# An encoder step on 8 cores: the first w_in chunk loaded as fp32 over a hardware queue and cast on chip, and three SBUF places exchanged

## What is computed

```python
# sub-layer 1: mixing
proj = rmsnorm(x, g_mix_pre) @ w_in            # (T, 2048) = [u | B | C | h], 4 x 512
y_pool = pool_mix(u)                           # trailing means over 2, 4, 8, 16 rows, minus u; then w_pool
y_conv = B * conv3(C * h)                      # causal depthwise convolution of width 3
x = x + rmsnorm(concat(group_rmsnorm(y_pool), group_rmsnorm(y_conv)) @ w_out, g_mix_post)
# sub-layer 2: cross-attention into 256 memory tokens, k = m @ w_k, v = m @ w_v
s = (rmsnorm(x, g_x_pre) @ w_q) @ k.T / 16
x = x + rmsnorm((softmax(s) @ v) @ w_co, g_x_post)
# sub-layer 3: squared-ReLU MLP
x = x + rmsnorm(relu(rmsnorm(x, g_ff_pre) @ w_up)**2 @ w_down, g_ff_post)
```

## Time and profile before

| | us |
|---|---|
| median of 3 runs | 855.21 |
| lowest and highest run | 854.38 and 895.62 |
| the profiled execution, its own time | 856.95 |
| its span (first to last instruction, slowest core, number 5) | 855.4 |
| spans of the eight cores in it | 846.5 to 855.4 |
| PE, DVE, ACT, POOL busy on core 5 | 816.9, 389.1, 389.9, 85.1 |

### The profile page before, as it was taken

The page is one execution under the profiler, slowest core; times in us unless marked ns, Lnnn a source line. Parts: engine busy times, 40 slices in busy tenths (PEclk is TensorE's granted clock), DMA queues, the critical chain, the costliest instruction groups (busy, mean ns, idle before and its releaser), DMA issues.

```text
span 855.4 us, 13864 instructions; the slowest of 8 cores (846.5 to 855.4 us)
## 1 busy us (share of the span) xinstructions
PE 816.9 (96%) x4724; PEld 393.0 (46%) x4724; DVE 389.1 (45%) x538; ACT 389.9 (46%) x806; POOL 85.1 (10%) x164
## 2 busy tenths in 40 slices
PE   2899999999998999999999999999999999999996
PEld 1444454544543455445554454444444444444442
DVE  3797885569774667665222222241122322222112
ACT  3596786858774657575332223332233401233111
POOL 7522103012100001000010000000000000000000
PEclk9999999999998999999999999999999999999998
DMA  8999349720299506993789816881248820294001
GB/s 190 196 221 217 129 142 209 116 37 1 33 146 144 192 12 211 159 174 76 147 143 159 188 60 145 151 149 51 98 105 150 157 57 25 65 154 77 25 25 49
DMA packets 29792, 102.38 MB, mean 120 GB/s; under 512 B 2386, under 2 KB 13266, under 8 KB 24348
## 3 DMA queue, kind: packets, MB, share of 16 engines
q0 software_dynamic: 19408, 67.32, 45.9%
q1 hardware_dynamic: 9740, 32.75, 11.1%
q10 hardware_dynamic: 576, 1.44, 0.6%
HBM read 144.38 MB, written 18.07 MB: 190 GB/s over the span
## 4 chain that ended last, share of the span: by engine, by line
PE 84%; DMA 11%; POOL 2%; issue 1%; DVE 1%; ACT 1%; POOLq 0%; DVEq 0%; ACTq 0%
PE ps L660 81%; DMA wdn_140<-w_down 4%; DMA wco<-w_co 4%; DMA win<-w_in 3%; PE ps L665 2%; DMA up_131<-w_up 1%; POOL sAB_101 L698 0%; POOL win L734 0%; DVE X L715 0%; DVE z_99 L715 0%; ACT rf_108 L689 0%; DVE Am L725 0%; POOL se_71 L727 0%; DVE O_55 L696 0%; DVE xT_53 L696 0%
## 5 line engine op out<-in xcount | busy, mean ns | idle before, releaser
L689 ACT ACTIVATE sqj<-ps 128x1024 bf16<-128x1024 f32 (+1 forms) x33 | 32.8, 995 | 176.4 <-PE ps L660 174.2
L660 PE MATMUL ps<-xT_53,win 128*128 128x512 bf16 x256 | 62.4, 385 | 17.7 <-DMA win<-w_in 16.6
L696 DVE TENSOR_TENSOR O_56<-ps,gp 128x1024 f32<-128x1024 f32 x24 | 29.3, 1222 | 97.7 <-PE ps L660 58.8
L696 DVE TENSOR_TENSOR O_55<-ps,gp 128x1024 f32<-128x1024 f32 (+1 forms) x25 | 29.5, 1178 | 95.4 <-PE ps L660 72.6
L689 ACT ACTIVATE rt_129<-ps 128x512 bf16<-128x512 f32 x64 | 38.2, 597 | 72.2 <-PE ps L660 69.3
L689 ACT ACTIVATE rt_128<-ps 128x512 bf16<-128x512 f32 x64 | 38.2, 597 | 70.3 <-PE ps L660 69.3
L660 PE MATMUL ps<-xT_54,win 128*128 128x512 bf16 x256 | 59.5, 379 | 0.6 <-DVE O_55 L696 0.6
L660 PEld LDWEIGHTS ps<-xT_53,win 128*128 128x128 bf16 x256 | 24.4, 99 | 46.1 <-issue 21.4
L660 PE MATMUL ps<-xT_54,up_130 128*128 128x512 bf16 x192 | 42.4, 379 | 0.0
L660 PE MATMUL ps<-xT_53,up_131 128*128 128x512 bf16 x192 | 42.4, 379 | 0.0
L660 PEld LDWEIGHTS ps<-xT_54,win 128*128 128x128 bf16 x256 | 24.8, 98 | 29.9 <-issue 0.8
(11 more groups left out here) (333 smaller groups left out, 1461.8 us busy)
## 6 DMA issues: line engine op xcount, KB each, us to landing
up_130<-w_up POOLq DMA_DIRECT2D x11, 1024.0 KB, 8.5
up_131<-w_up POOLq DMA_DIRECT2D x11, 1024.0 KB, 9.8
up_132<-w_up POOLq DMA_DIRECT2D x10, 1024.0 KB, 8.9
x<-X SPq DMA_DIRECT2D x16, 512.0 KB, 3.4
X<-x SPq DMA_DIRECT2D x16, 512.0 KB, 4.2
yp<-X SPq DMA_DIRECT2D x15, 512.0 KB, 2.6
X<-xp POOLq DMA_DIRECT2D x8, 512.0 KB, 44.0
X<-xp SPq DMA_DIRECT2D x8, 512.0 KB, 4.3
```

Source lines behind the costliest of these rows:

```text
L660: P.add([("pe", lambda e, L: e.matmul(L(out), lhsT=lhsT, rhs=rhs, start=start, stop=stop, skip_group_check=True), max(0.03, n * 0.000421 + ...
L689: return e.activation(out=L(out), in_=L(in_), func=func, scale=scale, **kw)
L696: opts.append(("dve", lambda e, L: e.tensor_tensor(out=L(out), in0=L(in0), in1=L(in1), op=op), c_dve(n, per)))
```

## The change

The first chunk of `w_in` is no longer loaded and cast by POOL's queue. It comes as fp32 over the SP queue into `Or[0]` and is cast into `win` by DVE or ACT, whichever the planner takes. The four XT loads change sides: 0 and 2 go over the ACT queue, 1 and 3 over SP. The second piece of `w_in` is emitted ahead of `Xe`. In the plan the engines are taken to be free from 0.6 us on, POOL from 3.5 us on. In cross-attention `Bm` moves to A0+56K, `wq` to 82K, `wco` to 40K (over chunks 8 to 15 of `win`), and `hid` 2 and 3, `wdn` 0 and 1 follow.

```diff
@@ schedule
-        free = {e: 0.0 for e in self.ENGS}
+
+        free = {e: 3.5 if e == "pool" else 0.6 for e in self.ENGS}
@@ build_program, SBUF places
-    Bm = at("Bm", A0 + 40 * K, 8 * D, BF16)
-    wq = at("wq", A0 + 56 * K, 8 * D, BF16)
-    wco = at("wco", A0 + 82 * K, 8 * D, BF16)
+    Bm = at("Bm", A0 + 56 * K, 8 * D, BF16)
+    wq = at("wq", A0 + 82 * K, 8 * D, BF16)
+    wco = at("wco", A0 + 40 * K, 8 * D, BF16)
...
-    hparts = [at("hid%d" % i, A0 + o * K, 8 * TN, BF16) for i, o in enumerate((72, 16, 40, 48))]
+    hparts = [at("hid%d" % i, A0 + o * K, 8 * TN, BF16) for i, o in enumerate((72, 16, 56, 64))]
...
-              for i, o in enumerate((A0 + 56 * K, A0 + 64 * K, W0, W0 + 8192, A0, A0 + 8 * K, A0 + 24 * K, A0 + 32 * K))]
+              for i, o in enumerate((A0 + 40 * K, A0 + 48 * K, W0, W0 + 8192, A0, A0 + 8 * K, A0 + 24 * K, A0 + 32 * K))]
@@ build_program, the first loads
-    load_win(0)
+    load(Or[0][:, :], win_d[0, :, 0:1024], 524288)
+    copy(win[:, 0:1024], Or[0][:, :], eng="act dve", per=0.56)
     for i in range(4):
-        load(XT[i], xt0[i], 524288, q=("sp", "act")[i % 2])
+        load(XT[i], xt0[i], 524288, q=("act", "sp")[i % 2])
     load_consts()
+    load_win(1)
     load(Xe[0:NX, :], xe[:, :], NX * 4096, q="pool")
-    load_win(1)
     load_wpool()
```

## The result

The changed kernel takes 861.43 us in the median of its runs (860.89 to 862.67), beside 854.8 for the kernel before on the same chip. The ratio is 1.0084, with a 95% interval of 1.0064 to 1.0103. Ratios and intervals leave out executions more than 1.5% above the fastest of the same kernel, such as the 895.62 of the kernel before. The forecast was 852.0 with a range of 846 to 857, so the time lies outside it, on the slower side. The profiled execution of the changed kernel took 862.67 us.

The account below looks back on a forecast made before the run. Core 5 sets the metric, losing 6.7 us at w_co; the start has several limits, then DVE carries it. Span 855.4 - 4.9 (places) - 0 (start) = 850.5, plus 1.55 around it, gives 852.0 us; range 846.0 to 857.0.

Parts of the forecast that it names:

- Places of w_co, w_q, Bm: Before `fold_b`: w_co issued at about 219 or 224, its wait gone on every core, metric 4.9 us lower.
- Forecast against the median: Whole kernel: 852.0 us against the median of 855.21, a gain of 3.2 us (0.4%).
- The gain of 4.9: Slowest core's span: core 5 loses its 6.7 us at w_co, core 2 becomes slowest, 855.4 - 850.5 = 4.9 us.
- The start at 0: First loads: `r0` and `U` 1.4 us later, covered by DVE's 1.43 us idle before 29.27; 0 gained.
- the start slips: Rival at the first loads: XT 2 lands at 20.7, stage starts 4.0 us later, 856.0 us; chance 0.16.
- the sign of that rival: At the start: `U` after 28 us would show that the start slips.
- issue order and plan times: Every engine's order after the new `free` times: unreadable from a trace, allowed 2 us either way.
- Something in the new order that none of these holds: Remaining case, anywhere in the new order, outside the forecast and its rivals; no size given, chance 0.06.
- an order that opens a long stall with its lower clock: Whole kernel: reason given for a result slower by more than about 2% (17 us); chance 0.03.
- The result within 2%: Whole kernel: time within about 2% (17 us), which a measurement can't tell from no change; chance 0.96.

Follow-up runs that it names:

- e12_add_first: Changed kernel with one exchange in VectorE's order, the first addition of squares ahead of the first scaling of XT 2: 862.66 us, ratio 1.0064 to the kernel before.

## Why the prediction was wrong, step by step

- **Places of w_co, w_q, Bm: right in mechanism, half in size.** The issue moved to 224.1 on core 5 (forecast 219 or 224). On the other cores of the changed kernel it is at 224.8 to 231.5, because all that stands ahead is late; with the places alone it is at 219.3 to 222.7 everywhere. The wait is gone on every core, the fold takes 7.1 us, and on core 5 the clock stays up. Forecast against the median was 0.4%; alone it gave 0.2% [0.07, 0.31]. The gain of 4.9 was read from the spans of one execution, in which core 5 happened to be the one that waits; another core is the slowest as soon as core 5 is mended.
- **The start at 0: right in the time, not in the chain.** Landings 7.2 and 16.7 forecast, 6.9 and 16.9 seen in the first uses on core 7; the cast took 0.72 us where 0.75 was taken from the earlier trace rows. New loads in the old order: 1.0002, with `U` at 26.4 in the median as forecast. The rival "the start slips" named XT 2 at 20.7, and this didn't come. But in the changed kernel's own order three additions follow XT 2 and not two, `U` comes at 27.6 in the median, and past 28 on two cores, which the prediction had named as the sign of that rival. The slip came from the order and not from XT; taking it back gained nothing (`e12_add_first`).
- **The step that failed is "issue order and plan times".** It was said that this can't be read from a trace, and then a bound of 2 us was put on it from the largest other waits, 1.0 us each. The new order alone measured 0.8% (1.0080), about 7 us. The bound was wrong in kind. A wait that is 1.0 us in an order that fits says nothing of the waits in one that doesn't: it is the order that keeps them at 1.0. In its place the runs showed two waits of PE: one of 2.0 us at 65 to 70 us on every core, behind a copy on DVE, and one of up to 3.6 us for w_v, each with some us of lower clock behind it on some cores. The row that could have warned is the one for w_v in the timeline of core 5: 18.6 us of landing with 19.1 until its use, so an order that takes a microsecond out of that interval opens a wait. The new one took out 0.8 to 1.5.
- **The chances.** "Something in the new order that none of these holds" had 0.06, and a chance of slower by the measurement's own bound was rated at 0.03. That last chance named the mechanism, "an order that opens a long stall with its lower clock", but only for a loss of over 2%. The result within 2% was rated 0.96, and that holds.

## What to carry to other kernels

Where a program plans its own order, an edit that adds one operation or moves one load is two changes: the edit, and a new order for everything. Hold the order to measure the first, redraw it a few times to size the second, and put the second in the forecast with its measured spread. Here seven orders made for the new loads gave ratios from 0.9997 to 1.0101. Look for transfers that land just in time (issue to use against issue to landing, core by core): with the slowest of eight cores as the metric, such a transfer is a loss in waiting.

## What the runs showed that I had not expected

The same load, at the same place of the program, lands after 17.0 to 21.7 us on the eight cores of one execution (the first half of w_v in the changed kernel), and which core is slow changes from run to run: core 7 waits 3.6 us in the changed kernel and not at all in the order held. There core 3 waits 2.7 for the second half, after it had already lost time at 60 us, and is the slowest by 4.8 us (855.2 beside 850.4). The metric takes the worst of eight such draws.
